# Moving the second activation tile and the weight residues inside the setup of a hybrid encoder trunk

## The reference, cut to what matters

```python
c_act = jax.nn.silu(c)
for layer in range(DEPTH):                              # DEPTH = 2
    mod = c_act @ ada_w[layer] + ada_b[layer]           # 1024 -> 3072
    shift, scale, gate = _split(mod, (D_MODEL, D_MODEL, D_MODEL))
    h = _rmsnorm(x, pre_g[layer]) * (1.0 + scale[:, None, :]) + shift[:, None, :]
    y = mixer(h)                                        # layer 0: z = h @ w_in, retention and latent attention
    x = x + gate[:, None, :] * _rmsnorm(y, post_g[layer])
```

## Time and profile before

| what | value |
|---|---|
| median of 3 runs | 2329.84 us (2329.31 to 2330.06) |
| the profiled execution: time of the device | 2329.45 us |
| its span from the first to the last instruction | 2327.7 us |
| TensorE busy | 2256.7 us, 97% of the span |
| VectorE, ScalarE, GpSimd busy | 59%, 49%, 39% |
| end of the stage `setup` | between 39.98 us (VectorE's last end) and 40.93 us (the first instruction of the next stage) |

### The profile page before, as it was taken

How to read it: one execution, slowest core, us unless ns; L and a number is a source line. 1 busy time by engine, 2 the same in 40 slices (tenths; PEclk the granted TensorE clock), 3 DMA queues, 4 the chain that set the end, 5 groups by cost and what they waited for, 6 DMA issues and landing times. The chain is left out here.

```text
span 2327.7 us, 32108 instructions
## 1 busy us (share of the span) xinstructions
PE 2256.7 (97%) x11426; PEld 1899.1 (82%) x11426; DVE 1377.4 (59%) x2098; ACT 1132.7 (49%) x2112; POOL 899.4 (39%) x666
## 2 busy tenths in 40 slices
PE   5999999999999999999999989998999999999998
PEld 5888888988887788888888878887888888888886
DVE  7333336434345667777676751215899999994442
ACT  5555534232223555555555545555555556654432
POOL 6322222222223201101010032322998999992454
PEclk9999998999999999999999999999999999999999
DMA  7533323443434313131221134331111111245553
GB/s 302 181 135 135 135 77 140 142 139 124 149 123 125 113 33 100 32 100 36 60 69 45 43 130 145 119 125 37 46 47 53 64 51 50 68 157 163 163 170 100
DMA packets 163857, 246.05 MB, mean 106 GB/s; under 512 B 8996, under 2 KB 111652, under 8 KB 159142
## 3 DMA queue, kind: packets, MB, share of 16 engines
q1 hardware_dynamic: 159142, 236.25, 30.9%
q10 hardware_dynamic: 4608, 8.39, 1.0%
HBM read 158.10 MB, written 86.51 MB: 105 GB/s over the span
## 5 line engine op out<-in xcount | busy, mean ns | idle before, releaser
L2357 POOL TENSOR_TENSOR conv_g<-conv_g,product 128x1024 f32<-128x1024 f32 x160 | 384.8, 2407 | 34.3 <-ACT product L2406 24.6
L2501 DVE SCALAR_TENSOR_TENSOR ps_b<-u,cols,ps_b 128x1024 f32<-128x1024 f32 x304 | 391.7, 1288 | 9.2
L2617 PE MATMUL ps_a<-ho_hi,wp_lo 128*128 128x512 f32 x768 | 301.0, 392 | 5.9 <-DVE h_left L2557 5.9
L2619 PE MATMUL ps_a<-ho_hi,wp_hi 128*128 128x512 f32 x768 | 300.4, 391 | 0.0
L2618 PE MATMUL ps_a<-h_left,wp_hi 128*128 128x512 f32 x768 | 300.1, 391 | 0.0
L2406 ACT ACTIVATE product<-u,cols 128x1024 f32<-128x1024 f32 x160 | 183.3, 1151 | 170.1 <-POOL conv_g L2357 168.8
L1719 DVE TENSOR_TENSOR pt_lo<-ps_pt,pt_hi 128x512 fp32r<-128x512 f32 x256 | 176.1, 688 | 135.9 <-ACT pt_hi L1610 133.7
L1610 ACT ACTIVATE pt_hi<-ps_pt 128x512 fp32r<-128x512 f32 x256 | 154.1, 603 | 203.3 <-PE ps_pt L1805 202.4
L1709 DVE TENSOR_REDUCE mx<-ps_s 128x1 f32<-128x512 f32 x248 | 168.0, 683 | 33.0 <-PE ps_s L1797 31.2
L1603 ACT ACTIVATE probs<-ps_s,bias 128x512 f32<-128x512 f32 x248 | 168.7, 700 | 15.0 <-PE ps_pt L1805 8.2
L2617 PEld LDWEIGHTS ps_a<-ho_hi,wp_lo 128*128 128x128 f32 x768 | 144.9, 189 | 37.6 <-DVE h_left L2557 7.8
(11 more groups left out here) (449 smaller groups left out, 5486.1 us busy)
## 6 DMA issues: line engine op xcount, KB each, us to landing
scratch_ret_pack<-pack SPq DMA_DIRECT2D x14, 1280.0 KB, 5.5
pack<-scratch_ret_pack SPq DMA_DIRECT2D x14, 1280.0 KB, 6.6
ada<-in_ada_w_dram SPq DMA_DIRECT2D x16, 768.0 KB, 5.8
wp_raw<-in_od_w_in_dram SPq DMA_DIRECT2D x24, 512.0 KB, 4.0
xt<-in_x_dram SPq DMA_DIRECT2D x16, 512.0 KB, 6.1
ada<-in_ada_w_dram SPq DMA_DIRECT2D x8, 1024.0 KB, 9.5
mix_e<-scratch_mix SPq DMA_DIRECT2D x16, 512.0 KB, 4.6
x_e<-in_x_dram SPq DMA_DIRECT2D x16, 512.0 KB, 5.2
```

Source lines behind the costliest of these rows:

```text
L2357: pool.tensor_tensor(half(conv_g, h), half(conv_g, h), product[adds(c, i, h) % 2][:], ALU.add).then_inc(added, 1)
L2501: dve.scalar_tensor_tensor(acc[h], units(c, k, h), params(c, k), acc[h], ALU.mult, ALU.add).then_inc(tap, 1)
L2617: pe.matmul(dst, lo[:, k, :], h_hi[:, k, t], start=k == 0, stop=False)
L2619: mm = pe.matmul(dst, hi[:, k, :], h_hi[:, k, t], start=False, stop=k == KD - 1)
```

## The change

Four things are moved, and no instruction is added or removed. In SyncE's program the load of x tile 1 moves from between the `ada_w` chunks 5 and 6 to behind the four first weight pieces. In ScalarE's program the square and the scaling of tile 1 move behind the four `w_hi` pieces. In VectorE's program the residues of pieces 1 and 2 move from ahead of the modulation's reductions to behind the making of `gain`, where that of piece 3 already is. GpSimd's and TensorE's programs are untouched.

```diff
@@ SyncE
             for k in range(KD):
-                if k == NW:
-                    sp.dma_start(xt[:, 1, :], x_pieces[1]).then_inc(x_ahead[1], 16)
                 if k >= NW:
                     sp.wait_ge(mod_sum, k - NW + 1)
                 sp.dma_start(ada[:, place(k), :], ada_view[k][:, 0:2 * D]).then_inc(ada_in[place(k)], 16)
             for k in range(KD // 2):
                 load_w(0, k, w0_in[k])
+            sp.dma_start(xt[:, 1, :], x_pieces[1]).then_inc(x_ahead[1], 16)
             for j in range(1, 3):
                 for k in range(KD // 2):
                     load_w(j, k, w_in[j])
@@ ScalarE
             act.activation(st.c_w[:].rearrange("p d h -> p (d h)"), expw[:], ACT.Exp).then_inc(a_step, 1)
+            for k in range(KD // 2):
+                at = slice(2 * k, 2 * k + 2), slice(0, BANK)
+                act.wait_ge(w0_in[k], 16)
+                act.activation(w_hi[:, *at], w_raw[:, *at], ACT.Copy).then_inc(whi_done, 1)
             act.wait_ge(x_ahead[1], 16)
             act.wait_ge(x0_turned, 1)
             act.activation(sq, xt[:, 1, :], ACT.Square, accum_out=ssq[1][:]).then_inc(sq_done, 1)
             act.wait_ge(rstd_done, 2)
             act.activation(xn[:], xt[:, 1, :], ACT.Copy, scale=rstd[1][:])
-            for k in range(KD // 2):
-                at = slice(2 * k, 2 * k + 2), slice(0, BANK)
-                act.wait_ge(w0_in[k], 16)
-                act.activation(w_hi[:, *at], w_raw[:, *at], ACT.Copy).then_inc(whi_done, 1)
             act.wait_ge(red_step, 5)
@@ VectorE
-            first_lo(1)
-            first_lo(2)
             dve.wait_ge(mod_first, 1)
@@
             dve.scalar_tensor_tensor(st.gain[:, layer, :], scale1[:], 1.0,
                                      st.cols[:, K_PRE + layer * KD:K_PRE + (layer + 1) * KD], ALU.add, ALU.mult)
-            first_lo(3)
+            for k in range(1, KD // 2):
+                first_lo(k)
```

## The result

The changed kernel takes 2338.9 us (median of 6 runs, 2337.09 to 2341.13), the kernel before 2329.35 us in the same measurement (6 runs). The ratio is 1.0042, with a 95% interval of 1.0029 to 1.0055: 0.42% or 9.8 us slower, where 8.7 us were forecast. The profiled execution took 2338.5 us, its span is 2336.7 us, 9.0 more than before.

What follows compares the result with a forecast made beforehand. VectorE's chain was taken to bound the setup (39.98), GpSimd 1.65 us behind. GpSimd's wait would end it at 48.7: 8.7 us on 2329.45 gives 2338.15, plus 0.39 to the median, 2338.5 us; range 2335.5 to 2340.3.

Steps and rivals of the forecast that it cites:

- The queue: Setup transfers: without tile 1's 512 KB ahead, `ada` chunks 6, 7 and four weight pieces land 1.23 us earlier; tile at 33.75.
- VectorE: Setup chain: `gain` at about 34.2, three residues of some 1.25 us, end at about 38.0, 2.0 us earlier.
- The wait in GpSimd's program: `norm(1)` inside the angle reduction: GpSimd waits about 10 us for ScalarE's later square, holding queued work that doesn't need tile 1.
- The size of it: GpSimd's end: square at 33.75, plus 2.17 to L300, plus 12.77 to L311's end, 48.69; setup 8.7 us later.
- the upper bound: GpSimd's stretch with VectorE's residues after 35.0 added in full (3.0 us): setup ends at 49.2, 9.2 later.
- The lower bound: GpSimd's stretch without VectorE: 12.77 less 2.50 for L307 and L309, 10.27 us; setup ends at 46.2, 6.2 later.
- The rival in which GpSimd runs free: Setup: VectorE doesn't hinder GpSimd's long instructions; 6.2 us later, 2336.0 us; chance 0.15 for 5.5 to 7.5 later.
- The range: Whole time: 2335.5 to 2340.3 us, from GpSimd's free and fully hampered ends with half of the clock's possible effect.
- Behind the setup: Next stage: everything moves by the setup's delay; TensorE's cold start counted as 0, though 1.6 us less or more possible.
- Tile 1 didn't overtake: Rival in the load queue: tile 1 overtakes weight pieces, VectorE stays last; 2.0 us earlier, 2327.8 us; chance 0.03.
- the delay wasn't hidden: Rival behind the setup: next stage waits less for its transfers; time within 0.2% of before, 2330 to 2334; chance 0.04.
- The rival with more than 10 us: Setup: GpSimd and VectorE could hamper each other on every instruction; 2341 us, chance 0.05.

Runs made afterwards that it cites:

- dve_only: The kernel before with only VectorE's residues of pieces 1 and 2 moved behind the making of `gain`; ratio 1.0005.
- x1_only: The kernel before with only tile 1's load and ScalarE's square and scaling of it moved behind the first weight pieces; ratio 1.0031, 7.2 us slower.
- act_order_only: The changed kernel with tile 1's load back between `ada` chunks 5 and 6, ScalarE still taking the weight pieces first; ratio 1.0041.
- norm_behind_angles: The changed kernel with GpSimd's `norm(1)` moved behind the angles, ahead of its weight residue; ratio 1.0003.
- residues_behind_angles: The changed kernel with one more wait: VectorE begins its three residues only when GpSimd has finished the angles; ratio 1.0051.
- residue_first: The changed kernel with GpSimd's weight residue ahead of the clamps and `norm(1)` last, and ScalarE's sine and cosine ahead of tile 1's scaling; ratio 1.0001.
- sine_first: The changed kernel with GpSimd's `norm(1)` behind the angles and ScalarE's sine and cosine ahead of tile 1's scaling; ratio 1.0003.

## Why the prediction was right, step by step

**The queue.** All of its steps came out within 0.05 us: VectorE's last product at 27.09 (forecast 27.07), ScalarE's first weight piece at 28.41 (28.4; 29.64 before), the square at 33.74 (33.75). 512 KB are worth 1.23 us of this queue, and the moved load gives that to all that stood behind it.

**VectorE.** It ends at 37.99 (forecast 38.0). Two small misses cancel in that: the three residues began 0.3 us later than forecast (34.51 for 34.2) and took 3.48 us, not 3 x 1.25. The 2.0 us are there and buy nothing. `dve_only` shows that they are not even VectorE's by right: with GpSimd running at that moment they are lost on an 8-column instruction.

**The wait in GpSimd's program.** This was the step that decided, and three runs bear it out: the late square alone brings most of the loss (`x1_only`), the loss is there with the tile loaded early as well (`act_order_only`), and moving the one call out of the angles removes it (`norm_behind_angles`). The wait was 10.99 us, where the forecast said about 10; its own numbers, 0.69 and the square's 10.36 us of delay, add up to 11.05.

**The size of it.** GpSimd ended at 49.56, not 48.69. Two terms were mis-sized, and they partly cancel. From the square to the start of L299 (L300 before) there were 37.37 - 33.74 = 3.63 us, not 2.17: L280 and L282 took 0.61 and 0.86 us longer beside VectorE's residues, a term that I had only in the upper bound. From there to the end there were 12.19 us, not 12.77, since only L299 was still hampered (0.48), where L309 had been before (2.55 against 1.50 alone). 1.46 - 0.58 = 0.88, and 0.87 is missing. That the forecast came this near is in part luck: keeping the old stretch of 12.77 us, with the old overlap in it, put too much into one place and nothing into the other.

**The lower bound was wrongly reasoned.** I put L307's 1.94 us down to VectorE, as L306, also with two operations on 512 columns, took 0.61. It takes 1.94 with VectorE idle and in either place. I also took L309 for half of L300, 1.38, where it takes 1.50 alone. The stretch without any stretched instruction is 11.70 us (35.96 to 47.66 in `x1_only`), not 10.27. The rival in which GpSimd runs free is thus 35.92 + 11.70 = 47.62, 7.6 us later and not 6.2. That is inside the 7.5 to 9.7 us that the prediction gave to its forecast, and the measured ratio's interval, 6.8 to 12.8 us, holds both. So the time alone can't tell the forecast from this rival; the rows of L280, L282 and L299 do. The rival had been priced from one pair of rows that looked alike.

**The range.** It doesn't follow the rule that the prediction gives for it. The free and the fully hampered end, 6.2 and 9.2 us later, with 0.8 us of clock to either side, are 2335.2 to 2339.8, where it has 2335.5 to 2340.3. The measured 2338.9 lies in both.

**Behind the setup.** The shift isn't quite rigid. At the first matmul it is 9.57 us. TensorE's timeline before:

```profile
51.87 0.48 PE L761 MATMUL ps_v<-w_hi,h_lo 128*128 128x512 f32 x1
...
58.40 0.47 PE L761 MATMUL ps_g<-w_hi,h_lo 128*128 128x512 f32 x1 [0.84 <-DVE w_lo L691]
```

And after:

```profile
61.85 1.03 PE L750 MATMUL ps_h<-const,xn 128*128 128x128 f32 x8
62.64 0.48 PE L758 MATMUL ps_v<-w_hi,h_lo 128*128 128x512 f32 x1
...
68.20 0.39 PE L758 MATMUL ps_g<-w_hi,h_lo 128*128 128x512 f32 x1
```

At `ps_v` it is 62.64 - 51.87 = 10.77 us. Of the first 24 matmuls 13 were spaced as at half clock (0.43 us) where 7 were before, and the rest 0.23 us. At `ps_g` it is 68.20 - 58.40 = 9.80. Before, TensorE stood there for 0.84 us for VectorE's `w_lo`; after, it came so late itself that it didn't have to wait. VectorE's `w_lo` moved by 9.56 us, no more than the stage did. So most of a longer cold start is taken back at this wait. From the first matmul to `ps_g` it is 14.40 us before and 14.63 in the changed kernel, and 14.40 to 14.78 over the ten profiles, though the cold start itself differs by 1.5 us. That is the term that I had set to 0 with 1.6 us to either side. At the end it is 9.0 us. Where the last 0.6 went isn't settled. The last `ps_qk` product with `h_lo` is still 9.5 apart (337.7 and 347.2). In the attention the first and the last `ps_s` product with `q_lo` are 7.9 and 8.2 apart (752.1 and 760.0, 1332.4 and 1340.6), and the first `ps_a` product with `wp_lo` 9.0 (1581.9 and 1590.9). So it changes in the stages with waits of TensorE in between, where the granted clock also differs from profile to profile (0.83 and 0.91 from 340 to 380). No run here isolated it.

**The other rivals.** Tile 1 didn't overtake (33.74), and the delay wasn't hidden. The rival with more than 10 us would have been the right one if VectorE's residues had met L310 too, as in `residues_behind_angles` (ratio 1.0051, 11.9 us).

No version beats the kernel before by an amount that can be measured. The change's idea ends at 39.89 at best here, against 39.98: with VectorE's 2 us taken out, GpSimd's and ScalarE's chains, which had 1.65 and 2.8 us of room, are the bound, and part of VectorE's and GpSimd's work can't run at the same time.

## What to carry to other kernels

When an operation is moved later on one engine, look up every other engine that waits for it, and read what stands behind that wait in its program: the cost is that queue, whether or not it needs the result. Before shortening the chain that ends last, note how much room the next ones have, since that bounds what there is to win (1.65 us here, for an edit that put 10 us into the neighbour). Price "without contention" from a run without it and not from two instructions that look alike.

## What the runs showed of the hardware

VectorE's instructions with two inputs in SBUF and GpSimd's instructions hold each other back, and how long depends on which is under way and what it does:

- VectorE's residues under way: GpSimd's next instruction is held. Its 1-column instructions took 0.80 and 1.43 us instead of 0.19 and 0.57 in the changed kernel, and L308 took 2.51 instead of 1.50 in `residue_first`.
- A `tensor_tensor` of GpSimd under way: VectorE is held to its end. An 8-column addition took 2.20 us behind a 2.36 us one of GpSimd (`dve_only`), and a residue 3.36 instead of 1.21 behind L310 (`residues_behind_angles`).
- A `tensor_scalar` of GpSimd under way: VectorE is held at its beginning at most. In `x1_only` L416 took 0.89 us right behind the start of L299, and then a whole residue of 1.22 us ran inside L299's 2.78. In `residue_first` one residue beside L308 took 1.63. In the kernel before, the first residue began at 32.08 inside L307 (31.45 to 33.39) and ended inside it, after 1.23 us. No run here shows why.

VectorE's products of the modulation, with one input in PSUM, took their 2.35 us beside GpSimd's 2.77 in every profile. The Trainium skill (GPSIMD Engine Reference, section Specifications) names contention with VectorE instructions that have two SBUF inputs; the traces agree, but not for the whole length of a `tensor_scalar`.

GpSimd's cost for a `tensor_scalar` on 512 columns depends on the operations: 0.61 us for min and max, 1.50 for one max, 1.94 for add and min.

The cold start of TensorE (its first matmuls of the stage, 0.43 us apart as at half clock, 1.2 GHz) differs from profile to profile and not with the time that it stood. From the first matmul to the turning of tile 1, 24 matmuls, it took 7.08 us before (after 9.96 us of standing), 8.28 in the changed kernel (20.40), 6.98 in `act_order_only` (20.46) and 8.43 in `sine_first` (11.03); over the ten profiles 6.92 to 8.43. The Trainium skill (TensorE: Matmul & The Clock Gate, section Part 1) says that the number of slow matmuls varies between runs of one kernel; the traces agree. In eight of the ten profiles the granted clock reads half there. In those of the changed kernel and of `residues_behind_angles` it reads full, though the matmuls start 0.43 us apart and later 0.23. Stretches of the changed kernel (length, busy time by engine, granted clock, DMA share, GB/s):

```profile
54.00:55.00 1.00, 1.00 (x3) 0.73 (x3) 0.60 (x2) 1.00 (x2) 0.67 (x1) 1.00 1.05 416
55.00:56.00 1.00, 1.00 (x4) 0.79 (x3) 0.00 (x0) 1.00 (x2) 1.00 (x1) 1.00 0.24 92
```

The same stretches of the kernel before, 44 to 47, have two and then four matmuls a us at a granted clock of 0.50. So the spacing of the matmuls is to be read beside the clock column.
